# Five projections of 1024 x 1024 as seven half-size products each, and four score groups in a row

## The reference

```python
def token_mixer(h, ...):                 # h: 256 x 1024, normalised x
    proj = h @ w_in                      # q, k/v of three attentions, x_m, o_pre, gates ...
    ...                                  # its last 2048 columns are gate_a and gate_b
    y_a = nsa_mixer(...)                 # 8 heads, 256 x 512
    y_b = mlstm_mixer(...)               # 4 heads, 256 x 512
    merged = sigmoid(gate_a) * (y_a @ w_up_a) + sigmoid(gate_b) * (y_b @ w_up_b)
    return merged @ w_o_mix

def memory_cross_attention(h, m, w_q, w_k, w_v, w_o):   # 4 heads of 256
    q, k, v = h @ w_q, m @ w_k, m @ w_v  # each 256 x 1024 by 1024 x 1024
    s = q k^T * 256 ** -0.5              # per head, 256 x 256
    p = softmax(s)
    return (p v) @ w_o

x = x + token_mixer(rmsnorm(x), ...)
x = x + memory_cross_attention(rmsnorm(x), rmsnorm(mem), ...)
x = x + moe_ffn(rmsnorm(x), ...)         # 32 experts, 12 MB of weights each, top 4
out = rmsnorm(x)
```

## Time and profile before

| what | us |
|---|---|
| median of 3 runs (lowest to highest) | 1278.0 (1276.98 to 1281.64) |
| span of the profiled execution | 1275.1 |
| PE busy in it | 1224.7 (96%) |
| DVE busy | 323.8 (25%) |
| ACT busy | 145.5 (11%) |
| experts' stage, first gather to end | from 363 to 1275 |

### The profile page before, as it was taken

The page is one execution under the profiler, slowest core; times in us unless marked ns, Lnnn a source line. Parts: engine busy times, 40 slices in busy tenths (PEclk is TensorE's granted clock), DMA queues, the critical chain, the costliest instruction groups (busy, mean ns, idle before and its releaser), DMA issues.

```text
span 1275.1 us, 14915 instructions
## 1 busy us (share of the span) xinstructions
PE 1224.7 (96%) x6165; PEld 601.4 (47%) x6165; DVE 323.8 (25%) x730; ACT 145.5 (11%) x325; POOL 7.9 (1%) x33
## 2 busy tenths in 40 slices
PE   9999999999999999999989999999998999999987
PEld 8868885858544333333333333433333344333322
DVE  2362324371733111212111111211111131211112
ACT  2223323002210000000000000000000000000001
POOL 1000000000000000000000000000000000000000
PEclk9999999999999999999999999999999999999999
DMA  9963233257499999999999999999999999999996
GB/s 331 310 217 132 87 112 132 99 214 277 162 368 427 428 427 427 427 428 430 429 428 428 428 430 428 429 428 430 429 429 428 428 426 428 428 428 428 428 426 267
DMA packets 61172, 454.69 MB, mean 357 GB/s; under 512 B 7309, under 2 KB 14153, under 8 KB 35145
## 3 DMA queue, kind: packets, MB, share of 16 engines
q1 hardware_dynamic: 58888, 452.49, 86.5%
q10 hardware_dynamic: 2240, 1.58, 0.4%
HBM read 453.00 MB, written 1.05 MB: 356 GB/s over the span
## 4 chain that ended last, share of the span: by engine, by line
PE 70%; DMA 28%; SPq 1%; DVE 1%; issue 1%; ACT 0%; DVEq 0%; ACTq 0%
PE ps L1399 32%; DMA r_odd<-in_w_gu_dram 16%; PE ps L920 13%; DMA ring<-in_w_down_dram 12%; PE ps L1249 4%; PE ps L927 3%; PE ps L1376 3%; PE ps L1392 3%; PE ps L1473 2%; PE ps L973 1%; PE ps L1504 1%; PE ps L1499 1%; PE ps L1320 1%; PE ps L1302 1%; SPq L520 1%
## 5 line engine op out<-in xcount | busy, mean ns | idle before, releaser
L1399 PE MATMUL ps<-ring,r_memT 128*64 128x512 f32 x1024 | 225.8, 594 | 13.1 <-DMA ring<-in_w_gu_dram 12.4
L1399 PE MATMUL ps<-r_odd,r_memT 128*64 128x512 f32 x1024 | 225.4, 594 | 12.5 <-DMA r_odd<-in_w_gu_dram 12.3
L1399 PE MATMUL ps<-ring,r_kx 128*64 128x512 f32 x768 | 176.7, 609 | 12.5 <-DMA ring<-in_w_down_dram 12.5
L2104 DVE TENSOR_SCALAR r_ga<-ps 128x512 f32<-128x512 f32 x32 | 22.1, 692 | 635.6 <-PE ps L1399 635.6
L1399 PEld LDWEIGHTS ps<-r_odd,r_memT 128*64 128x64 f32 x1024 | 72.9, 137 | 162.4 <-issue 135.6
L1399 PEld LDWEIGHTS ps<-ring,r_memT 128*64 128x64 f32 x1024 | 71.9, 137 | 161.3 <-issue 135.6
L920 PE MATMUL ps<-r_odd,ring 128*128 128x256 f32 x576 | 128.0, 380 | 0.0
L1399 PEld LDWEIGHTS ps<-ring,r_kx 128*64 128x64 f32 x768 | 55.0, 140 | 131.2 <-issue 108.6
L920 PEld LDWEIGHTS ps<-r_odd,ring 128*128 128x128 f32 x576 | 108.5, 190 | 16.7 <-issue 2.3
L861 ACT ACTIVATE r_ga<-r_ga 128x512 f32<-128x512 f32 x32 | 20.1, 630 | 459.9 <-DVE r_ga L2104 459.9
L1376 PE MATMUL ps<-r_dm,r_x 128*128 128x128 f32 x512 | 65.8, 282 | 0.0
(11 more groups left out here) (358 smaller groups left out, 827.5 us busy)
## 6 DMA issues: line engine op xcount, KB each, us to landing
ring<-in_w_gu_dram SPq DMA_DIRECT2D x60, 2048.0 KB, 27.4
r_odd<-in_w_gu_dram SPq DMA_DIRECT2D x60, 2048.0 KB, 27.9
ring<-in_w_down_dram SPq DMA_DIRECT2D x46, 2048.0 KB, 22.6
r_gbx<-in_w_down_dram SPq DMA_DIRECT2D x15, 2048.0 KB, 28.5
ring<-in_w_in_dram SPq DMA_DIRECT2D x7, 2048.0 KB, 13.9
r_odd<-in_w_gu_dram SPq DMA_DIRECT2D x8, 1024.0 KB, 15.1
ring<-in_w_gu_dram SPq DMA_DIRECT2D x8, 1024.0 KB, 7.2
ring<-in_w_k_x_dram SPq DMA_DIRECT2D x2, 2048.0 KB, 11.1
```

Source lines behind the costliest of these rows:

```text
L1399: last = mm(ps[n * SLOTS:(n + 1) * SLOTS, bk, :], stationary_, moving(n), start=start, stop=stop, skip_group_check=True)
L2104: V.tensor_scalar(gact, ps[:, GBK, :], 7.0, None, ALU.min).then_inc(g_limited, 1)
```

## The change

`ga`, `gb`, `kx`, `vx` and `qx` are each computed by seven half-size products: with the token matrix in quarters a11 a12 / a21 a22 (rows are the two blocks of 128 tokens, columns the two halves of the features) and the weights in b11 b12 / b21 b22,

P1 = a11 b11, P2 = a12 b21, P3 = s3 b22, P6 = s1 b11', P5 = s0 b22', P7 = s2 b12', P4 = a22 b21',

with s0 = a21 + a22, s2 = a11 - a21, s1 = s0 - a11, s3 = a12 - s1, and b12' = b22 - b12, b11' = b12' + b11, b21' = b21 - b11', b22' = b22 - b11'. Each primed quarter is written over its old content in the ring, once that has been read: b11' waits for the end of P1, b21' for that of P2, b22' for that of P3.

In `ga`, `gb`, `kx`, `qx` a product is 16 matmuls of 128 x 128 stationary by 128 moving columns; in `vx` it is 4 matmuls with 512 moving columns. P1, P6, P7 and P4 of a matrix accumulate in one bank that is held for them (P6, P7, P4 start on top of what is there), so that each of them waits until the state before has been copied out; P2, P3, P5 are added by DVE. The other groups of the loop have five banks in turn instead of six. The products are dealt out to the loop's turns (two a step) as `TURNS` says. DVE gets four 128 x 2048 operations on the weights and four 128 x 512 additions per matrix, and three times four 128 x 512 sums of tokens. ACT copies P1, P3, P7, P4 and, for the gates, takes the tanh in place afterwards; its copies of the first turn of a step now stand behind the scaling of the probabilities. `rows` moves to `r_ga`, the mLSTM weights `wm` to `r_gb`, and `r_kx` and `r_hT` hold the token sums. Both halves of a weight matrix are now released by P4 and P7, near the matrix's end. In the cross attention all query products stand ahead of the four score groups, and `pt0` behind them.

```diff
-FILL = [("ga", n) for n in range(4)] + [("gb", n) for n in range(4)] + \
-       [("kx", n) for n in range(4)] + [("vx", n) for n in range(4)]
+WIDE = ("ga", "gb", "kx", "vx")
+HELD = (1, 6, 7, 4)
+TURNS = [(1, 2), (3, 6), (5, 7), (4,)] * 3 + [(1, 2), (3,), (6, 5), (7,), (4,)]
...
-    g += ["qx0", "qx1", "sx0", "qx2", "sx1", "qx3", "sx2", "pt0", "sx3"]
+    g += [f"qxP{n}" for n in QUERY] + ["sx0", "sx1", "sx2", "sx3", "pt0"]
...
+        if name in held:
+            pairs.append((name, BANKS - 3))
+            continue
...
-        n = BANKS - 2 if first <= i < last else BANKS
+        n = BANKS - 3 if first <= i < last else BANKS
...
+            def wide_product(w, n):
...
+                tokens, weight = {1: (a11, b11), 2: (a12, b21), 3: (made[:, 3], b22), 6: (made[:, 1], b11),
+                                  5: (made[:, 0], b22), 7: (made[:, 2], b12), 4: (a22, b21)}[n]
...
+                elif n == 3:
+                    weights(f"{w}1")
+                    pe.wait_ge(token_sums_ready, 1 + i // 2)
+                elif n != 2:
+                    pe.wait_ge(wide_sums, 4 * i + {7: 1, 6: 2, 4: 3, 5: 4}[n])
+                o = begin(f"{w}P{n}")
+                for c in range(1 if w == "vx" else 4):
+                    for k in range(4):
+                        first, final = c == 0 and k == 0 and n not in HELD[1:], k == 3
+                        if w == "vx":
+                            last = mm(o, tokens[:, k], weight[:, k], start=first, stop=final, skip_group_check=True)
+                        else:
+                            last = mm(o[:, c * P:(c + 1) * P], weight[:, k, c * P:(c + 1) * P], tokens[:, k],
+                                      start=first, stop=final, skip_group_check=True)
+                end(f"{w}P{n}", last)
...
-            cross_query(0)
-            cross_query(1)
-            cross_scores(0)
-            cross_query(2)
-            cross_scores(1)
-            cross_query(3)
-            cross_scores(2)
+            for n in (1, 2, 3, 6):
+                cross_query(n)
+            cross_query(5, range(2))
+            cross_query(7)
+            cross_query(5, range(2, 4))
+            cross_query(4)
+            for h in range(HX):
+                cross_scores(h)
             cross_turn(0)
-            cross_scores(3)
...
+            def difference_of_right(w):
...
+                V.tensor_tensor(b12, b22, b12, ALU.subtract).then_inc(wide_sums, 1)
...
+            def sum_over_first(w):
...
+                filled_of(dve, f"{w}P1")
+                V.tensor_tensor(b11, b12, b11, ALU.add).then_inc(wide_sums, 1)
...
+            def lower_differences(w):
...
+                filled_of(dve, f"{w}P2")
+                V.tensor_tensor(b21, b21, b11, ALU.subtract).then_inc(wide_sums, 1)
+                filled_of(dve, f"{w}P3")
+                V.tensor_tensor(b22, b22, b11, ALU.subtract).then_inc(wide_sums, 1)
...
+            def products_added(turn):
...
+                    elif n == 6:
+                        filled_of(dve, f"{w}P6")
+                        drained_of(dve, f"{w}P3")
+                        drain(f"{w}P6", added(w, 0, 1, 6))
...
             V.tensor_tensor(gelT.rearrange("p g k j -> p (g k j)"), hidT, hid2, ALU.mult).then_inc(gelu_done, 1)
+            difference_of_right("ga")
...
+                    if h == 4:
...
+                        token_sums(sums_m, memT)
...
+                    if h % 2 == 0:
+                        sum_over_first(WIDE[h // 2])
+                    products_added(2 * h)
...
+                if h < HA:
+                    if h % 2 == 0:
+                        lower_differences(WIDE[h // 2])
+                    products_added(2 * h + 1)
+                    if h % 2 and h < HA - 1:
+                        difference_of_right(WIDE[h // 2 + 1])
...
+                if n == 2:
+                    for piece_ in ("qx0", "qx1"):
+                        dve.wait_ge(loaded[slot_of[piece_]], need[piece_])
+                    b11, b12, b21, b22 = query_blocks()
+                    V.tensor_tensor(b12, b22, b12, ALU.subtract).then_inc(query_sums, 1)
```

More of the change, by code:

```diff
@@ L1078, in _ @@
                             end(("csA", "csB")[half], last)
[L1080 to L1105, removed]
-                        drained_of(pe, f"te{m}")
[L1107 to L1112, removed]
+            def wide_product(w, n):
+                i = WIDE.index(w)
+                src, made = (hT, sums_h) if i < 2 else (memT, sums_m)
+                a11, a12, a21, a22 = token_blocks(src)
+                b11, b12, b21, b22 = wide_blocks(w)
+                tokens, weight = {1: (a11, b11), 2: (a12, b21), 3: (made[:, 3], b22), 6: (made[:, 1], b11),
+                                  5: (made[:, 0], b22), 7: (made[:, 2], b12), 4: (a22, b21)}[n]
+                if n == 1:
+                    weights(f"{w}0")
+                    for m in range(4 if i >= 2 else 0):
+                        drained_of(pe, f"te{m}")
+                elif n == 3:
[7 more added lines that the diff above has]
+                        first, final = c == 0 and k == 0 and n not in HELD[1:], k == 3
+                        if w == "vx":
+                            last = mm(o, tokens[:, k], weight[:, k], start=first, stop=final, skip_group_check=True)
+                        else:
+                            last = mm(o[:, c * P:(c + 1) * P], weight[:, k, c * P:(c + 1) * P], tokens[:, k],
+                                      start=first, stop=final, skip_group_check=True)
+                end(f"{w}P{n}", last)
@@ L1113, in _, with wide_turn @@
+            def wide_turn(turn):
+                for w, n in wide_products(turn):
+                    wide_product(w, n)
             for h in range(HA + 1):
@@ L1288, in _, with cross_query @@
             project_and_turn("om", "om", sga, "tx", lambda k: pe.wait_ge(merged_ready, k // 2 + 1), 0)
[L1290 to L1295, removed]
+            def cross_query(n, part=range(4)):
+                a11, a12, a21, a22 = token_blocks(hT)
+                b11, b12, b21, b22 = query_blocks()
+                tokens, weight = {1: (a11, b11), 2: (a12, b21), 3: (sums[:, 3], b22), 6: (sums[:, 1], b11),
+                                  5: (sums[:, 0], b22), 7: (sums[:, 2], b12), 4: (a22, b21)}[n]
+                if n < 3:
+                    weights("qx1")
+                    for m in (2 * n - 2, 2 * n - 1):
+                        drained_of(pe, f"tx{m}")
+                elif n == 3:
+                    weights("qx0")
+                    pe.wait_ge(query_tokens, 1)
+                else:
+                    pe.wait_ge(query_sums, {7: 1, 6: 2, 4: 3, 5: 4}[n])
+                o = begin(f"qxP{n}") if part[0] == 0 else bank(f"qxP{n}")
+                for c in part:
+                    for k in range(4):
+                        last = mm(o[:, c * P:(c + 1) * P], weight[:, k, c * P:(c + 1) * P], tokens[:, k],
+                                  start=(c == 0 and k == 0 and n in (1, 2, 3, 5)), stop=(k == 3), skip_group_check=True)
+                if part[-1] == 3:
+                    end(f"qxP{n}", last)
             def cross_scores(h):
-                drained_of(pe, f"qx{h}")
+                for n in (6, 5) if h < 2 else (2, 4):
+                    drained_of(pe, f"qxP{n}")
                 o = begin(f"sx{h}")
@@ L1674, in _ @@
+            for n in range(4):
+                drained_of(dve, f"tm{n}")
+            token_sums(sums_h, hT)
             filled_of(dve, "vec")
```

180 lines of the change are left out of this document (128 added, 52 removed).

## The result

The changed kernel took 1269.3 us (median of four runs, 1268.3 to 1270.2), the kernel before 1277.5 us (1277.0 to 1281.6): a ratio of 0.993 (0.992 to 0.994). The span of the profiled execution fell from 1275.1 to 1266.6 us, by 8.5 us. The forecast was 1268.0 us. In a second comparison of the same two kernels the ratio was 0.9935 (0.9922 to 0.9949).

The account below looks back on a forecast made before the run. PE was taken to bound the kernel up to 363 us, the experts' weight transfers after: 14.0 us less PE work minus 4.0 us of stalls takes the span from 1275.1 to 1265.1 us, median 1268.0, range 1263.0 to 1277.0.

Parts of the forecast that it names:

- The bound: Before 363 us PE sets the pace, then the experts' weights; a microsecond saved before moves the whole rest forward by one.
- transfers eat the gain: Rival, experts' stage: its transfers start at a time not tied to PE, gain ends as weight waits; 1278 us, chance 0.05.
- The record's price: Half-size products: 111.6 ns per 128-column record, so 25.00 us a matrix instead of 27.64, saving 2.64 us each.
- The loop: Attention loop: 8.5 us shorter, with PE stalls in `vx` only.
- The waits of `vx`: Loop steps 6 and 7: PE waits for DVE 1.6 us before P5 and 1.3 us before P7, 2.9 us.
- Slack in `ga`, `gb`, `kx`: Loop: b22' is ready before P5 by 0.6 us in `ga`, about 2 us in `gb` and `kx`; no stall.
- stalls everywhere: Rival, loop: each of the four matrices loses 2.9 us as `vx` does; 1276.7 us, chance 0.17.
- Queries and scores: Cross attention: 1.1 us of the 2.6 saved is lost in waits before `pt1` to `pt3`, `ox0` and `ox1`.
- Five banks in turn: PSUM banks, five instead of six: each group's predecessor is copied out more than 2 us before, so no cost.
- edits at nothing: Token sums, b12' of `ga` and `qx`, longer-held ring pieces, five banks: all hidden, costing no time.
- The sum: Whole kernel: 14.0 us less PE work, 4.0 us new stalls, 10.0 us gained before 363 us; span 1265.1 us.
- The step from span to median: Whole kernel: median of the runs stays 2.9 us above the profiled span, giving 1268.0 us.

Follow-up runs that it names:

- e6_delay: The changed kernel with 45 unused matmuls on PE ahead of the output projection; 1278.8 us, ratio 1.0007 to the kernel before.
- r_both: Second run of the changed kernel with both the bank-deal edit and the DVE/ACT order edit; 1266.7 us, ratio 0.9912 to the kernel before.
- e1_banks: The changed kernel with only the PSUM bank deal moved on by four behind `roP1`; 1267.6 us, ratio 0.9925 to the kernel before.
- e4_before_banks: The kernel before with only the bank deal moved on by four from `roP1`, putting `tf3` in bank 0; 1280.2 us, ratio 1.0031.
- e2_order: The changed kernel with only DVE's and ACT's lists of steps 6 and 7 reordered; 1266.1 us, ratio 0.9906 to the kernel before.
- e3_both: The changed kernel with both the bank-deal edit and the DVE/ACT order edit, first run; 1266.0 us, ratio 0.9903 to the kernel before.
- e8_queries: The changed kernel with queries and scores as in the kernel before; 1272.6 us, ratio 0.9960 to the kernel before.

## Where the prediction was right, and where it was wrong

**The bound: right, to a microsecond or two.** What PE lost before the first gather, the kernel lost (`e6_delay`), and the experts' stage was 911.6 us in the profiles of both kernels. The case that transfers eat the gain falls, since the 8.5 us by which the first gather came earlier are all in the span. For the last microsecond of a larger gain this is not shown: of the 3.9 of `r_both` 2.8 came through.

**The record's price: right.** 111.6 ns were taken from one row of 32 records; the 224 of the queries take 112.0 ns, those of `ga` (99.59 - 85.20 for 128 records) 112.4. Neither 108 nor the 123.4 ns at which the change would have gained nothing is what it costs. The ratio of the Trainium skill (TensorE: Matmul & The Clock Gate, Back-to-back issue gap), by which I had estimated 160 ns, is not borne out for float32. A matrix in the loop costs 25.1 to 25.3 us instead of 25.00, but the whole product cost 27.7 to 27.9 there instead of 27.64, so the saving of 2.6 us is the one forecast. (For 108 ns the prediction gives 3.3 us more; 896 records of 3.6 ns are 3.2.)

**The loop: 8.0 us won, 8.5 forecast.** 0.3 of the 0.5 missing stand before P4 of `vx`, which waits for ACT's copy of P7: ACT takes 0.60 us for it from 214.72 us, so P4 can begin at 215.3 at the earliest, while the transposes of that place take 0.66 from 214.52. I had put the copy beside the transposes, at nothing. Another 0.1 is that the products of `vx` alone save 3.4 us and not 3.5 (24.3 without the waits, 27.7 before). The rest, some 0.1, lies in pieces too small to name.

**The waits of `vx`: right.** 1.6 and 1.3 us were forecast. From P6's start to P5's it is 5.08 us where the product alone takes 3.44, so 1.6; from P5's to P7's 4.66, so 1.2. Both are released by DVE as named, and both go when the order does. DVE's timeline of the changed kernel has the walk: the last of the mLSTM's work, b21', b22' up to 206.30, then step 7's list with a copy, masks and maxima (left out here), and only behind them the additions of P6 and P5 in one row.

```profile
200.77 1.13 DVE L2009 TENSOR_SCALAR r_odd<-r_odd,vT 128x256 f32<-128x256 f32 x4
201.82 2.28 DVE L1772 TENSOR_TENSOR ring<-ring 128x2048 f32<-128x2048 f32 x1
204.02 2.28 DVE L1774 TENSOR_TENSOR ring<-ring 128x2048 f32<-128x2048 f32 x1
206.22 0.41 DVE L1929 COPY r_x<-ps 128x256 f32<-128x256 f32 x1
...
210.18 1.48 DVE L1778 TENSOR_TENSOR r_odd<-r_odd,ps 128x512 f32<-128x512 f32 x2
```

**Slack in `ga`, `gb`, `kx`: right in sign.** 0.6 us were read off for `ga`, 1.0 it was; 2 us for `gb` and `kx`, 1.7 it was. The rival of stalls everywhere had its condition not met: it needed one of 2.9 us in each, and even 2.0 us more on DVE make one of 1.1, in `ga` alone. DVE's load in the loop was forecast as 50 us beside the 52 and came to 95: b12' of `ga`, 2.3 us, falls ahead of the loop, and DVE no longer copies the four quarters of `vx` out, 2.8 us.

**Queries and scores: 1.1 us of waits forecast, 0.6 measured.** The mis-sized term is the distance between two heads. I had put it at 2.5 us, with the next head's maximum behind the reciprocal and its exponential behind both. ACT's timeline of the changed kernel:

```profile
304.03 0.56 ACT L881 ACTIVATE r_odd<-ps,sm 128x256 f32<-128x256 f32 x1 [0.76 <-DVE sm L2131]
...
305.46 0.91 ACT L890 ACTIVATE r_odd<-r_odd,sm 128x256 f32<-128x256 f32 x2 [0.23 <-DVE sm L2135]
306.28 0.55 ACT L881 ACTIVATE r_odd<-ps,sm 128x256 f32<-128x256 f32 x1
...
307.69 0.91 ACT L890 ACTIVATE r_odd<-r_odd,sm 128x256 f32<-128x256 f32 x2 [0.23 <-DVE sm L2135]
308.51 0.55 ACT L881 ACTIVATE r_odd<-ps,sm 128x256 f32<-128x256 f32 x1
```

The heads' scalings follow 2.23 us apart. ACT scales one head while DVE takes the next one's maximum, and the next exponential begins right behind the scaling, with no bracket: the maximum lies beside ACT's work, not in the chain. From the first `pt` to `ro` PE takes 317.36 - 308.08 = 9.28 us for work of 4 x 0.43 + 4 x 1.73 = 8.6 us, so some 0.6 are lost. Of these 0.5 lie before the first `ox` (309.47 - 308.08 = 1.39 us for two `pt` of 0.43) and 0.1 behind it; `pt2` and `pt3`, for which waits on ACT were forecast, follow without one, and the one bracket names DVE's copy for `ox0`.

**"Five banks in turn": the step that failed.** It stands among the edits at nothing, with "walking the list, each group's predecessor in its bank is copied out more than 2 us before". I walked the groups of the loop and of the queries, which the diff touches. There the step held: no wait there is one for a bank dealt in turn. The diff also changes how many groups there are, and the deal behind them goes on from another bank. At the residual products, which have fixed banks and wait for whatever was dealt there last, that made 1.4 us (`e1_banks`, `e4_before_banks`). The row that showed the exposure was in the trace of before, in a place I did not look at:

```profile
353.22 0.66 PE L1283 MATMUL ps<-ident,r_x 128*128 128x128 f32 x4 [0.35 <-DVE r_x L1921]
353.71 1.88 PE L1345 MATMUL ps<-r_x,ident 128*128 128x512 f32 x4
```

The residual product follows the last `tf` at once, and the norm that copies `tf3` is still to come.

The sum then: 10.0 us forecast and 10.0 measured up to `ro`; 1.5 lost behind it; span 1266.6 where 1265.1 was forecast. The errors of 0.5 us in the loop and in the queries cancelled, so that sum is better than its terms. The step from span to median, 2.9 us forecast and 2.7 found, is luck in part. Time and span of one and the same execution are 1.7 to 1.9 us apart in every run; the rest comes from profiled executions that were fast ones, the fastest of four for the changed kernel and close to the fastest for the kernel before.

## To carry to other kernels

Where a planner deals a resource in turn, write its deal out before and after for the whole list, not for the groups that the diff touches; look at each place with a fixed bank, and at who was dealt there last. When an edit doubles the work of an engine with a fixed order, its share of busy time says little: walk its list against the engine it feeds, since here a load of 95 us in 137 made no wait with a bracket on PE in the loop where the order was good, and 2.9 us of waiting where it was not. What a product of half the size costs is to be read from rows of that size, since 216 ns did not halve to 108 but to 112, and a quarter of the eighth was gone with that.

## What the runs showed that was not expected

**The clock fell in two executions though PE was busy.** In `e2_order` and in `e3_both` the granted clock was 0.57 from 84 to 88 us, nearer to the 1.2 GHz level than to that of 2.4, and 1.00 in the ten other profiles. `e2_order`, from 79 to 88 us (columns as above), and below it `r_both`, whose code is that of `e3_both`:

```profile
79.00:84.00 5.00, 5.00 (x82) 4.68 (x84) 2.71 (x9) 2.28 (x5) 0.00 (x0) 1.00 0.71 253
84.00:88.00 4.00, 4.00 (x25) 3.19 (x24) 3.06 (x14) 0.65 (x2) 0.00 (x0) 0.57 0.57 212
```

```profile
79.00:84.00 5.00, 5.00 (x74) 4.13 (x72) 3.16 (x8) 2.28 (x5) 0.00 (x0) 1.00 0.61 199
84.00:88.00 4.00, 4.00 (x43) 3.62 (x44) 2.66 (x10) 0.63 (x1) 0.00 (x0) 1.00 0.75 280
```

PE was busy all of the 5 us before in both, with products of 15 and 128 columns on 64 rows. In `e2_order` it cost 1.6 us: 0.9 in a score group (2.43 us start to start in place of 1.49) and 0.7 in the products behind it. `e3_both` lost as much. Why it fell in these two and not in the others, one of them with the same code, is open.

**The experts' stage is not quite constant.** From the first gather to the end it took between 911.6 and 914.0 us in twelve profiles with the same code there, the longest in `e3_both` and `e8_queries`. In `e3_both` 2.1 us are one wait for a transfer. I found no relation to the edits ahead of it or to when the stage begins. It is as large as the effects of `e1_banks` and `e2_order`, and it is why what is said of them rests on rows and not on times.
